# Two transformer blocks in one kernel: a raw place more in the ring of weights, a place fewer for their first halves

## The reference

```
h = rms_norm(x, ln1);  proj = h @ w_in
y_a = gated_deltanet(...) @ w_branch_a
y_b = moba_attention(...) @ w_branch_b
x = x + (sigmoid(gate_a) * y_a + sigmoid(gate_b) * y_b) @ w_out
u = causal_dwconv(rms_norm(x, ln2) @ w_up)
x = x + (silu(u_gate) * u_val) @ w_down
x = rms_norm(x, final_norm)
for l in range(2):
    shift, scale, gate = split(silu(c) @ w_mod[l] + b_mod[l], 3)
    h = rmsnorm(x, norm_gain[l]) * (1 + scale) + shift
    proj = h @ w_in_2[l]
    y_a = sparse_attention(q_a, k_a, v_a, q_i, k_i, w_i, positions, rel_bias) * silu(g_a)
    y_b = head_groupnorm(retention(rotary(q_b), rotary(k_b), v_b)) * silu(g_b)
    x = x + gate * (concat(y_a, y_b) @ w_out_2[l])
```

## Time and profile before

| what | value |
|---|---|
| runs | 1892.87, 1889.32, 1898.02 us; median 1892.87 |
| profiled execution | 1896.64 us, span 1894.8 us |
| DVE SCALAR_TENSOR_TENSOR for second halves in `ring`, first halves in `w1` | 483 of 1234 ns |
| ACT ACTIVATE for their first halves | 483 of 1057 ns |
| sums of `w_mod` chunks from `ring` on DVE | 135 of 1308 ns |
| a chunk of 512 KB from issue to landing | 5.1 to 6.1 us |
| read from HBM | 531.50 MB, 282 GB/s over the span |

### The profile page before, as it was taken

How to read it: one execution, slowest core, us unless ns; L and a number is a source line. 1 busy time by engine, 2 the same in 40 slices (tenths; PEclk the granted TensorE clock), 3 DMA queues, 4 the chain that set the end, 5 groups by cost and what they waited for, 6 DMA issues and landing times.

```text
span 1894.8 us, 33593 instructions
## 1 busy us (share of the span) xinstructions
PE 1827.1 (96%) x13102; PEld 1709.5 (90%) x13102; DVE 1682.1 (89%) x2239; ACT 1246.4 (66%) x1963; POOL 94.6 (5%) x72
## 2 busy tenths in 40 slices
PE   6999999999999998999999999999899999999998
PEld 5889899999998898989998997999789889988997
DVE  7888997977898799999999898899898979998896
ACT  6667754744665675656666676866577867667783
POOL 0000031031000001122000000000000000000000
PEclk9999998999999998999999999999999999999999
DMA  8887876868999896889899997888789878877995
GB/s 289 263 291 245 289 235 223 299 211 280 308 361 334 296 312 234 277 292 310 291 323 339 338 321 244 298 270 259 238 286 325 276 245 315 249 268 247 336 313 181
DMA packets 258523, 535.81 MB, mean 283 GB/s; under 512 B 23608, under 2 KB 28733, under 8 KB 257341
## 3 DMA queue, kind: packets, MB, share of 16 engines
q1 hardware_dynamic: 257933, 531.44, 82.8%
q10 hardware_dynamic: 432, 2.23, 0.3%
HBM read 531.50 MB, written 2.10 MB: 282 GB/s over the span
## 4 chain that ended last, share of the span: by engine, by line
PE 45%; DVE 14%; issue 3%; ACT 2%; DMA 1%; DVEq 0%; ACTq 0%
PE ps L152 44%; DVE ring_r L1954 5%; DVE AR_r L1954 2%; DVE macc L1954 1%; DVE AR L1946 1%; DVE stg L1954 1%; DMA ring<-in_w_in 1%; ACT w L1500 1%; DVE stg L1946 1%; DVE AR L1954 1%; ACT stg L1506 1%; ACT AR L1500 0%; DVE AR L2435 0%; DMA ring<-in_w_out 0%; DVE sm L2431 0%
## 5 line engine op out<-in xcount | busy, mean ns | idle before, releaser
L1954 DVE SCALAR_TENSOR_TENSOR ring_r<-ring,w 128x1024 fp32r<-128x1024 f32 x483 | 585.3, 1234 | 79.6 <-ACT w L1500 78.0
L1500 ACT ACTIVATE w<-ring 128x1024 fp32r<-128x1024 f32 x483 | 500.8, 1057 | 179.8 <-PE ps L152 80.2
L152 PE MATMUL ps<-hh_r,w 128*128 128x256 f32 x3480 | 503.4, 288 | 2.7 <-DVE hlo L1954 2.4
L152 PEld LDWEIGHTS ps<-hh_r,w 128*128 128x128 f32 x3480 | 451.1, 191 | 11.0 <-issue 8.1
L152 PE MATMUL ps<-hlo,ring_r 128*128 128x256 f32 x3108 | 435.4, 283 | 0.1
L152 PEld LDWEIGHTS ps<-hlo,ring_r 128*128 128x128 f32 x3108 | 399.1, 189 | 0.5 <-DVE ring_r L1954 0.5
L1954 DVE SCALAR_TENSOR_TENSOR AR_r<-AR,w 128x1024 fp32r<-128x1024 f32 x146 | 177.7, 1231 | 27.1 <-ACT w L1500 26.7
L152 PE MATMUL ps<-AR 128*128 128x64 f32 (+5 forms) x1320 | 180.0, 296 | 12.3 <-DVE AR L1950 6.1
L152 PEld LDWEIGHTS ps<-AR 128*128 128x128 f32 (+1 forms) x1320 | 163.3, 195 | 21.7 <-issue 11.9
L1500 ACT ACTIVATE w<-AR 128x1024 fp32r<-128x1024 f32 x146 | 152.3, 1057 | 45.7 <-PE ps L152 19.0
L1954 DVE SCALAR_TENSOR_TENSOR macc<-ring,sm,macc 128x1024 f32<-128x1024 f32 x135 | 176.6, 1308 | 1.0 <-DMA ring<-in_w_mod 0.5
(11 more groups left out here) (226 smaller groups left out, 2222.8 us busy)
## 6 DMA issues: line engine op xcount, KB each, us to landing
ring<-in_w_in SPq DMA_DIRECT2D x313, 512.0 KB, 5.1
ring<-in_w_mod SPq DMA_DIRECT2D x145, 512.0 KB, 5.6
ring<-in_w_up SPq DMA_DIRECT2D x124, 512.0 KB, 5.4
ring<-in_w_out SPq DMA_DIRECT2D x66, 512.0 KB, 5.6
ring<-in_w_down SPq DMA_DIRECT2D x66, 512.0 KB, 6.1
AR<-in_w_in SPq DMA_DIRECT2D x64, 512.0 KB, 5.7
AR<-in_w_up SPq DMA_DIRECT2D x52, 512.0 KB, 5.6
AR<-in_w_mod SPq DMA_DIRECT2D x34, 512.0 KB, 5.1
```

Source lines behind the costliest of these rows:

```text
L152: return e.matmul(o, l, x, start=start, stop=stop, skip_group_check=True)
L1500: return e.activation(o, i, ACT.Copy, scale=scale)
L1954: return e.scalar_tensor_tensor(o, a, s, b, op0, op1)
```

## The change

One of the six places for first halves becomes a tenth raw place; both are a chunk in size.

```diff
-R1 = 9
-R2 = 6
+R1 = 10
+R2 = 5
```

## The result

The changed kernel takes 1904.4 us (median of 10 runs, 1901.8 to 1909.8) against 1896.3 for the kernel before (10 runs, 1889.3 to 1901.6): a ratio of 1.0052, with a 95% interval of 1.0038 to 1.0067. It is slower by half a percent. The forecast was 1883.1 and its range ended at 1900: wrong in sign, and outside the range.

The account below looks back on a forecast made before the run. PE was taken as the bound, losing time mainly where it waits for DVE. Gains of 15.5 less losses of 5.7 give 9.8 us off 1892.9: 1883.1 us, range 1868 to 1900.

Parts of the forecast that it names:

- The sooner sends: A raw place more lets SP send each chunk one chunk sooner; taken as nothing in the sum.
- The rival of 5.7 more: Three weight transfers in the chain, sent sooner, each give up to 1.9 us: 1877.4 us; chance 0.14.
- The norms, 3.8 and 1.9: Fewer halves made ahead: PE loses 3.8 us at the third norm and 1.9 at the fourth.
- The eight gains, 15.5: At eight stops of PE, splits or sums moving behind the awaited DVE step save 15.5 us together.
- 3.6 at 599: PE's wait for the sum modend reads: 1.9 us filled by one more chunk, 1.7 from the clock staying up.
- 1.2 at 733: One split goes behind the bias step PE waits for: 1.2 us, or 2.9 if the slow split moves.
- 1.2 at 1151: The split at 1149.49 goes behind the second half of the FFN activation PE waits for: 1.2 us.
- 2.7 at 1344: Two sums at 1338.64 go behind the reciprocal: 2.7 us of a stop of 6.65.
- 2.5 at 1409: A sum and a split leave the front of the awaited step: 2.5 us, all of the stop.
- 3.0 at 1735 and 1745 together: One split moved at 1735 gives 1.2 us; a split and a sum moved at 1745 give 1.8.
- The losses outside the norms: Halves coming one chunk, 1.9 us, later elsewhere: covered in nearly all stretches, so nothing in the sum.
- slower: the halves run out: PE waits for second halves where DVE is busiest, 1.9 us in six stretches: 1910.0 with no gains; chance 0.12.

Follow-up runs that it names:

- e1: Kernel before with one place for first halves taken away and no raw place given (nine raw, five for first halves): 1907.3 us, ratio 1.0060.
- e7: Kernel before (nine raw places, six for first halves) with an unused stretch taken out and the tile of small values denser: 1891.3 us, ratio 0.9985.
- e2: Kernel before with only a raw place added (ten raw, six for first halves), room made by a denser memory layout: 1888.2 us, ratio 0.9969.
- e5: Changed kernel with sums put back: every w_mod chunk one place earlier in the list, splits left as changed; 1897.2 us, ratio 1.0003.
- e6: Kernel before with only the w_mod sums moved: every w_mod chunk one place later, splits keeping their place; 1910.7 us, ratio 1.0074.
- e4: Nine raw places, steps ordered as for five first-half places, but halves dealt over six real places after planning: 1906.9 us, ratio 1.0057.
- norms: Kernel before with one part of hlo not lent for first halves ahead of the third and fourth norm: 1888.1 us, ratio 0.9968.
- sums_some: Changed kernel with w_mod chunks one place earlier only in four parts of the list, whose stretches had lost: 1893.2 us, ratio 0.9987.

## Why the prediction was wrong

It named the mechanism that decides, steps changing their place in DVE's list, and gave it the wrong sign in sum. Point by point:

- **No work and no traffic are added: right.** DVE's busy time is 1680.2 for 1682.1.
- **The sooner sends are worth nothing: right within 3 us** (e1 against the changed kernel, e7 against e2), though ACT's waits for landings fall from 52.9 us in e7 to 19.4 in e2. The rival of 5.7 more was too high.
- **The norms, 3.8 and 1.9: right in the mechanism and the waits.** PE waits 3.74 for the fifth chunk and 1.85 for the sixth. That the third norm's stretch grew by just 3.9 has some luck in it: the norm's first multiplication comes 0.8 us sooner in its stretch, which was taken as nothing, and the eight behind the wait took 1.88 us, where 1.21 is usual.
- **The eight gains, 15.5: wrong, 4.5 came.** 1.4 of 3.6 at 599 (the stop shrank to 0.75, and still the clock was 0.72 from 603 to 609, as behind the stop of before, so the 1.7 for the clock didn't come; and that stretch varies by 3 us by itself); minus 1.6 for 1.2 at 733; 1.9 for 1.2 at 1151; 0.8 for 1.3 at 1306; 1.9 for 2.7 at 1344; 0.4 for 2.5 at 1409 (3.0 gained, 2.6 lost in the next stretch); minus 0.3 for 3.0 at 1735 and 1745 together.
- **The losses outside the norms: taken as nothing, and they were some 21 us in the traces, clock included.** This is the step that failed. Putting the sums alone back takes 7 us off the changed kernel's time (9 by the ratios).

The failing step can be quoted: "So everywhere one split, and often one or two `w_mod` sums, that stood ahead of such a step on DVE now stands behind it." It is true, and I counted each such move as a gain, "limited to what moved", at the places where PE stood still before. Two things are missing there. First, what leaves the front of one step lands in front of the next one, or another sum takes its place. At 733 the changed kernel shows it:

```profile
728.80 1.28 DVE L1954 SCALAR_TENSOR_TENSOR macc<-ring,sm,macc 128x1024 f32<-128x1024 f32 x1
730.00 2.92 DVE L1954 SCALAR_TENSOR_TENSOR AR_r<-AR,w 128x1024 fp32r<-128x1024 f32 x1
732.85 1.21 DVE L1954 SCALAR_TENSOR_TENSOR ring_r<-ring,w 128x1024 fp32r<-128x1024 f32 x1
733.98 0.74 DVE L1950 TENSOR_SCALAR AR<-AR,cst 128x1024 f32<-128x1024 int32 x1
```

A split did go behind the bias step at 733.98, but a sum of 1.28, which before stood further ahead (725.35), now comes between at 728.80, and the slow split of 2.92 stayed. Second, a stop that exists can shrink, a stop that doesn't exist can only appear. Going through the stops of the profile before, I looked at a list that holds possible gains and no possible losses. At 177, 478, 1436 and 1658 that trace had little or no stop, because a sum happened to fill DVE's wait for ACT or had been done in time; for the last three e5 and e6 show that it was the sums. The reading of the lines at 1650 to 1664 shows how for one of them.

The rival "slower: the halves run out" had the right sign and a wrong mechanism. It put 1.9 us into each of the stretches where DVE is busiest. The longest of these, 843 to 1139, takes 295.3 us in both kernels. Halves did run out at the place that the rival named, 1403 (a wait of 1.44 for `ring_r`, and 1.09 for `w` at the end of the block), which is 2.5 us of the 21. But with the sums put back (e5) PE's waits at these places are 0.21, 0.61 and 0.22, so even there the larger part is the sums'. And e4, which has the sixth place and e1's time, shows no loss by the missing place itself.

The fourth norm lost 2.4 with the changed kernel's order and 1.5 in norms, sums_back and sums_some. PE's wait is the same (1.84 or 1.85); the rest is clock, 0.97 over the stretch and 1.46 us for the eight multiplications behind the wait, against 1.00 and 1.21.

What stays open: how the loss at 174-205 divides between splits, sums and clock; and where the changed kernel loses its 9 us in the runs whose clock is as good as that of the kernel before, since the one traced had 0.981.

## What to carry to other kernels

Where an engine works through a list in order, moving an item isn't worth its duration. Ask what the engine does in the time that comes free (it may be waiting for another engine, with the moved item as its only filler), and what the item delays where it lands. Look for the losses in the places that have no stop yet: those where an item that needs nothing from others fills a wait. And where a planner turns a size into an order, test the size and the order apart: give the chip the place back and keep the order, or shift one kind of step only.

## What the runs showed of the hardware that I had not expected

- The same multiplications went 5% faster when `ring` and `w1` had moved down by 448 bytes per partition: eight of 256 columns every 0.905 us for 0.95, at a granted clock of 1.00. With weights in `AR`, itself moved by 640 bytes, it took 0.96, hardly another time than before. Which address matters wasn't tried.
- A stop of 1.16 us at 479.88 was followed by half clock (2.05 us for eight multiplications), and one of 1.44 at 1405.68 was not (1.19 for four). The length of a stop alone doesn't tell whether the clock falls, and it can fall with no stop at all. PE before:

```profile
183.34 2.48 PE L152 MATMUL ps<-cst,macc 128*128 128x1 f32 x16
185.69 2.05 PE L152 MATMUL ps<-hh_r,w 128*128 128x256 f32 x8
```

and in "norms", at the same steps:

```profile
182.89 1.93 PE L152 MATMUL ps<-cst,macc 128*128 128x1 f32 x16
184.67 1.20 PE L152 MATMUL ps<-hh_r,w 128*128 128x256 f32 x8
```

PE ran on in both, through 24 matmuls of one column, and the clock fell to half in one execution and not in the other. So a term for the clock taken from one place and one execution, as at 599, is a guess for another.
